# First layer of a two-block model on one core: projections in pairs of seven products, angles on GpSimd

## The reference, cut to what matters

```
hn = rmsnorm(x, norm_g)
q, k, v, u, z_a, z_b = split(hn @ w_in)            # each 1024 wide
o_a = chunked_relpos_attention(q, k, v, rel_bias) * silu(z_a)     # 16 heads of 64
y   = gelu(s5_ssm(u, ...))        # diagonal complex recurrence: a rotation by an angle and a decay
o_b = y * sigmoid(y @ w_glu + b_glu) * silu(z_b)
x   = x + concat(o_a, o_b) @ w_out
```

## Time and profile before

| | |
|---|---|
| median of 3 runs | 2581.97 us (2581.15 to 2583.98) |
| the profiled execution | 2580.91 us, its span 2579.2 us |
| busy: PE, PE weight load, DVE, ACT, POOL | 99%, 95%, 67%, 24%, 13% |
| loop of the first layer, with its start and the gate matrix behind it | the first 420 us |

### The profile page before, as it was taken

The page is one execution under the profiler, slowest core; times in us unless marked ns, Lnnn a source line. Parts: engine busy times, 40 slices in busy tenths (PEclk is TensorE's granted clock), DMA queues, the critical chain, the costliest instruction groups (busy, mean ns, idle before and its releaser), DMA issues.

```text
span 2579.2 us, 57925 instructions
## 1 busy us (share of the span) xinstructions
PE 2553.5 (99%) x22218; PEld 2458.9 (95%) x22218; DVE 1720.6 (67%) x3630; ACT 612.3 (24%) x1557; POOL 341.5 (13%) x479
## 2 busy tenths in 40 slices
PE   8999999999999999999999999999999999999998
PEld 7888889989999999999999999999999999999997
DVE  7667667565555556788998954655655655777855
ACT  3222221121001112234334320211211012344311
POOL 0111110010001100143443410211220000000000
PEclk9999999999999999999999999999999999999999
DMA  6444433444444444434334435343343444444443
GB/s 255 146 146 138 142 135 130 166 144 168 167 159 149 160 163 164 163 132 163 150 143 163 150 119 197 134 162 132 131 144 151 163 170 172 169 157 164 178 164 114
DMA packets 63764, 400.71 MB, mean 155 GB/s; under 512 B 6816, under 2 KB 13488, under 8 KB 17584
## 3 DMA queue, kind: packets, MB, share of 16 engines
q1 hardware_dynamic: 62992, 397.20, 41.8%
q0 software_dynamic: 672, 2.11, 0.5%
HBM read 397.17 MB, written 2.11 MB: 155 GB/s over the span
## 4 chain that ended last, share of the span: by engine, by line
PE 94%; DVE 3%; issue 2%; ACT 1%; DVEq 0%; DMA 0%; POOL 0%; SPq 0%; ACTq 0%; POOLq 0%
PE psum L607 68%; PE psum L551 12%; PE psum L560 2%; PE psum L1085 1%; PE psum L582 1%; PE psum L778 1%; PE psum L1094 1%; PE psum L690 1%; PE psum L871 1%; PE psum L988 1%; PE psum L842 1%; PE psum L1046 1%; PE psum L683 0%; PE psum L592 0%; PE psum L718 0%
## 5 line engine op out<-in xcount | busy, mean ns | idle before, releaser
L607 PE MATMUL psum<-h,ring 128*128 128x128 f32 x4384 | 524.3, 275 | 1.9 <-DVE near L1797 1.9
L607 PEld LDWEIGHTS psum<-h,ring 128*128 128x128 f32 x4384 | 506.6, 192 | 2.4 <-DVE wide_c L2304 2.0
L607 PE MATMUL psum<-mix,ring 128*128 128x128 f32 x3994 | 477.7, 275 | 0.4
L607 PEld LDWEIGHTS psum<-mix,ring 128*128 128x128 f32 x3994 | 461.4, 192 | 1.4 <-DVE near L1790 1.3
L551 PE MATMUL psum<-h,ring 128*128 128x256 f32 x1504 | 336.1, 381 | 0.0
L551 PEld LDWEIGHTS psum<-h,ring 128*128 128x128 f32 x1504 | 281.7, 190 | 45.7 <-issue 9.4
L1797 DVE TENSOR_TENSOR near<-psum,near 128x128 f32<-128x128 f32 x143 | 41.3, 289 | 344.9 <-PE psum L607 344.9
L607 PE MATMUL psum<-ring,h 128*128 128x128 f32 x1296 | 153.8, 275 | 0.6 <-DVE near L1797 0.6
L607 PEld LDWEIGHTS psum<-ring,h 128*128 128x128 f32 x1296 | 149.1, 192 | 0.7 <-issue 0.7
L1757 DVE TENSOR_TENSOR ring<-ring 128x1024 f32<-128x1024 f32 x112 | 137.9, 1231 | 0.0
L1154 ACT ACTIVATE w<-psum 128x128 f32<-128x128 f32 x75 | 20.8, 277 | 469.8 <-PE psum L607 469.8
(11 more groups left out here) (494 smaller groups left out, 4029.9 us busy)
## 6 DMA issues: line engine op xcount, KB each, us to landing
ring<-w_out SPq DMA_DIRECT2D x80, 1024.0 KB, 5.1
ring<-w_odd SPq DMA_DIRECT2D x64, 1024.0 KB, 4.9
ring<-w_hgrn SPq DMA_DIRECT2D x64, 1024.0 KB, 5.4
ring<-w_even SPq DMA_DIRECT2D x48, 1024.0 KB, 4.8
ring<-w_nsa SPq DMA_DIRECT2D x48, 1024.0 KB, 5.5
ring<-w_rg SPq DMA_DIRECT2D x40, 1024.0 KB, 5.4
ring<-w_cmp_in SPq DMA_DIRECT2D x8, 1024.0 KB, 4.8
ring<-w_rgg SPq DMA_DIRECT2D x10, 512.0 KB, 6.9
```

The lines of the kernel that those rows point to most:

```text
L607: mm = pe.matmul(dst, stationary, moving, start=new and j == 0, stop=new and j == kh - 1, skip_group_check=not new)
```

## The change

It touches the first layer's loop alone.

- **PE.** q with k, and z_a with z_b, become two pairs in seven products (`fast_e`), u and v stay whole. In turn 0 only the gates are such a pair; q and k are whole products there (`from_x`), taken from the raw input and scaled afterwards by DVE. The order of a turn is u (first half), the values' weighting of the turn before, u (second half), pair q/k with the read-outs of the turn before behind its first product and the drives behind its second, pair z_a/z_b with the scores behind its second product and the first head's turning behind its sixth, the second head's turning, v.
- **Banks.** The pairs take banks 0, 1, 2. u goes to bank 2, v to bank 1, drives and heads from bank 2 to bank 7, and the read-outs from bank 7 into the upper half of bank 5. So the read-outs now wait for `o_used` of their turn as well, DVE's read of the attention output in bank 5.
- **DVE** gets per turn eight forms and ten additions, and gives up the angles, the small inputs and the skip product. The forms of q/k for the next turn are made at the turn's end, behind `states(3)`. The four sums of activations are made once, into x, which is loaded again (2 MB) while the gate matrix runs.
- **POOL** gets the small inputs, the skip product (u times a column), a factor of 8 on the bias, and the angles of the next turn, between its parts of state 1 and of state 2. The angle formula uses wide_b's lower half only (its upper half now holds a form) and has one instruction more.
- **ACT** gets four reads of banks instead of four copies, the sines now stand at the turn's start and the gelu's tanh inside the q/k pair.
- **Loads.** The weights of v go to slot 10, a part of mix; z_a and z_b to slots 3 and 4.

The loop of POOL, new:

```diff
+            def angles(turn, seen):
+                y = wide_b[:, 0:4, :]
+                arg = wide_a[:, :, :].rearrange("p (t c) n -> p t c n", c=2)
+                st.mark(g.tensor_copy(cur[:, 8:12], s5[:, 1, ds(4 * turn, 4)]))
+                g.wait_ge(trig_ready, after(seen))
+                st.settle()
+                apart(g)
                 for t in range(4):
-                    g.wait_ge(rot_used, after(4 * i + t + 1))
-                    g.wait_ge(y_ready, after(4 * i))
-                    g.tensor_tensor(states5(t, 0), w8[:, 0, :], w9[:, 1, :], ALU.add).then_inc(state_ready, 1)
-                    g.tensor_tensor(states5(t, 1), w9[:, 0, :], w8[:, 1, :], ALU.subtract).then_inc(state_ready, 1)
+                    st.mark(g.tensor_scalar(y[:, t, :], ccol("time"), cur[:, 8 + t:9 + t], None, ALU.mult))
+                st.settle()
+                apart(g)
+                st.mark(g.tensor_scalar(arg[:, :, 0, :], y, ROUND, -ROUND, ALU.add, ALU.add))
+                st.mark(g.tensor_scalar(arg[:, :, 1, :], y, 0.25, ROUND, ALU.add, ALU.add))
+                st.settle()
+                st.mark(g.tensor_tensor(arg[:, :, 0, :], y, arg[:, :, 0, :], ALU.subtract))
+                st.mark(g.tensor_scalar(arg[:, :, 1, :], arg[:, :, 1, :], -ROUND, None, ALU.add))
+                st.settle()
+                g.tensor_tensor(arg[:, :, 1, :], arg[:, :, 1, :], y, ALU.subtract).then_inc(phase_ready, 1)
+            def state(i, t):
+                g.wait_ge(rot_used, after(4 * i + t + 1))
+                g.wait_ge(y_ready, after(4 * i))
+                g.tensor_tensor(states5(t, 0), w8[:, 0, :], w9[:, 1, :], ALU.add).then_inc(state_ready, 1)
+                g.tensor_tensor(states5(t, 1), w9[:, 0, :], w8[:, 1, :], ALU.subtract).then_inc(state_ready, 1)
+            def turn_inputs(i):
+                g.wait_ge(landed[6], even1.loads[3].land0 + i * even1.loads[3].land_per)
+                st.mark(g.tensor_copy(cur[:, 12:20].rearrange("p (c t) -> p c t", c=2), s5[:, 2:4, ds(4 * i, 4)]))
+                st.mark(g.tensor_copy(slope[:, 0:1], pcol("d_skip")[:, ds(i, 1)]))
+                bias = ring[:, 6, 512:1024]
+                st.mark(g.tensor_scalar(bias, bias, 8.0, None, ALU.mult))
+                st.settle()
+                apart(g)
+                st.mark(g.memset(ring[0:64, 6, 512 + 192:768], NEG))
+                g.memset(ring[0:64, 6, 768 + 192:1024], NEG).then_inc(bias_masked, 1)
+                c_mat = ring[:, 6, T:2 * T].rearrange("p (c t n) -> p c t n", c=2, t=4)
+                coef = cur[:, 12:20].rearrange("p (c t) -> p c t", c=2)
+                for n, (part, by) in enumerate(((0, 0), (1, 1), (0, 1), (1, 0))):
+                    st.mark(g.tensor_tensor(c_tmp[:, n, :].rearrange("p (t n) -> p t n", t=4), c_mat[:, part],
+                                            coef[:, by, :].unsqueeze(2).to_broadcast([P, 4, 32]), ALU.mult))
+                g.wait_ge(u_ready, after(i + 1))
+                g.wait_ge(y_used, after(i))
+                st.settle()
+                apart(g)
+                g.tensor_scalar(skip[:, :], uT[:, :], slope[:, 0:1], None, ALU.mult).then_inc(skip_made, 1)
+                st.mark(g.tensor_tensor(c_in[:, 0, :], c_tmp[:, 0, :], c_tmp[:, 1, :], ALU.subtract))
+                g.tensor_tensor(c_in[:, 1, :], c_tmp[:, 2, :], c_tmp[:, 3, :], ALU.add).then_inc(c_in_ready, 1)
+            def even_turn(i, last):
+                turn_inputs(i)
+                state(i, 0)
+                state(i, 1)
+                if not last:
+                    angles(i + 1, i + 1)
+                state(i, 2)
+                state(i, 3)
             g.wait_ge(con_in, 16)
+            g.wait_ge(s5_made, after(1))
+            angles(0, 0)
+            with g.Fori(0, PAIRS - 1) as i:
+                st.enter(i, 18)
+                even_turn(i, False)
+                st.leave(PAIRS - 1)
+            even_turn(PAIRS - 1, True)
             g.wait_ge(cum_made, after(1))
```

The turn of PE, new:

```diff
+            def gate_pair_and_values(i):
+                block_products(fast_e, i, 1, of_h, sums_even, 4, None, ((u_ready, after(i + 1)),),
+                               ((2, lambda: scores(i)), (6, lambda: turn_head(i, 0))))
+                turn_head(i, 1)
+                pe.wait_ge(later_read, after(5 * fast_e.number(i, 1) + 4))
+                values(even1, i, 6, bank[1])
+            def even_turn(i):
+                pe.wait_ge(later_read, after(5 * fast_e.number(i, 0)))
+                product(even1, i, 0, bank[2], 0, 8)
+                mix_values(i - 1)
+                product(even1, i, 0, bank[2], 8, KT)
+                block_products(fast_e, i, 0, of_h, sums_even, 4, None, ((v_ready, after(i)),),
+                               ((1, lambda: read_outs(i - 1)), (2, lambda: drives(i))))
+                gate_pair_and_values(i)
             def glu_block(b, k0, k1):
...
-            pair(PAIRS - 1, True)
+            unscaled(lambda k: tile(even1, 0, k), bank[2][:, 0:T], raw, 0)
+            from_x(even1, 1, bank[0], 6)
+            from_x(even1, 2, bank[1], 1)
+            drives(0)
+            pe.wait_ge(h_ready, after(KT))
+            gate_pair_and_values(0)
+            with pe.Fori(1, PAIRS) as i:
+                even_turn(i)
+            last = PAIRS - 1
+            pe.wait_ge(y_mixed, after(last))
+            pe.wait_ge(first_read, after(2 * EVEN))
+            wait_load(pe, glu, 0, 0)
+            glu_block(0, 0, 7)
+            mix_values(last)
+            glu_block(1, 0, 7)
+            read_outs(last)
+            pe.wait_ge(bu_used, after(4 * PAIRS))
+            wait_load(pe, glu, 0, 1)
```

What PE's hooks hold, and the slots:

```diff
+            def read_outs(i):
+                pe.wait_ge(c_in_ready, after(i + 1))
+                pe.wait_ge(y_used, after(i))
+                pe.wait_ge(o_used, after(i + 1))
+                pe.wait_ge(state_ready, after(8 * i + 8))
+                for c in range(2):
...
-        even1 = Phase(PAIRS, 6, [Load(n, tiles("w_even1", n), SLOT, n + 1) for n in range(4)] +
-                      [Load(6, None, 0, 6, 2)] +
-                      [Load(n, tiles("w_even1", n), SLOT, n + 1) for n in range(4, 6)])
+        even1 = Phase(PAIRS, 16, [Load(0, tiles("w_even1", 0), SLOT, 1), Load(1, tiles("w_even1", 1), SLOT, 7),
+                                  Load(2, tiles("w_even1", 2), SLOT, 8), Load(6, None, 0, 16, 2),
...
+        fast_e = Fast(even1, ((1, 2, None), (4, 5, None)), 8, 0, True, 1)
...
+            if ph is glu:
+                sp.wait_ge(used, done(even1, PAIRS - 1, 15))
+                sp.dma_start(x[:, :, :], a["xT"].rearrange("k p t -> p k t")).then_inc(x_back, 16)
```

The turn of DVE, new, cut to its order (`states` is unchanged but for a wait on the sines at its start; its last two products still wait for POOL's half of the state before, `v.wait_ge(state_ready, after(8 * i + 2 * t))`):

```diff
+            def even_turn(i, first, last):
+                then(v.tensor_copy(cur[:, 0:4], s5[:, 0, ds(4 * i, 4)]))
+                if not first:
+                    first_sum(fast_e, i, 0)
+                states(i, 0)
+                if not first:
+                    two_sums(fast_e, i, 0, q_and_k)
+                    three_forms(fast_e, i, 1)
+                    fourth_sum(fast_e, i, 0, q_and_k)
+                    fifth_sum(fast_e, i, 0, q_and_k)
+                states(i, 1)
+                first_sum(fast_e, i, 1)
                 v.wait_ge(bias_masked, after(i + 1))
...
+                fourth_form(fast_e, i, 1)
+                two_sums(fast_e, i, 1, z_in)
...
+                fourth_sum(fast_e, i, 1, z_in)
+                states(i, 2)
+                fifth_sum(fast_e, i, 1, z_in)
+                states(i, 3)
+                if not last:
+                    three_forms(fast_e, i + 1, 0)
                 v.wait_ge(za_tanh, after(i + 1))
...
+                if not last:
+                    fourth_form(fast_e, i + 1, 0)
                 v.wait_ge(za_used, after(i + 1))
                 v.wait_ge(o_ready, after(i + 1))
...
                 v.wait_ge(y_ready, after(4 * i + 4))
+                v.wait_ge(skip_made, after(i + 1))
+                v.tensor_tensor(w4[:, 0, :], bank[5][:, T:2 * T], skip[:, :], ALU.add).then_inc(y_used, 1)
...
+            for n, (unit, sem, times) in enumerate(((7, first_read, 2), (8, later_read, 5))):
+                v.wait_ge(used, done(even1, 0, unit))
+                v.tensor_tensor(q_and_k[:, n, :], bank[n][:, 0:T], rstd[:, :], ALU.mult).then_inc(sem, times)
+            v.wait_ge(h_ready, after(KT))
+            sums(sums_even, h[:, 0:8, :], h[:, 8:16, :], 0, made=even_sums)
+            v.sem_inc(forms_made, 2)
+            three_forms(fast_e, 0, 1)
+            even_turn(0, True, False)
+            with v.Fori(1, PAIRS - 1) as i:
+                st.enter(i - 1, 38)
+                even_turn(i, False, False)
+                st.leave(PAIRS - 2)
+            even_turn(PAIRS - 1, False, True)
```

More of the change, by code:

```diff
@@ L26 @@
 PAIRS = 8
+EVEN = 2 * PAIRS
 HEADS = 16
@@ L509, in fill @@
                         sp.wait_ge(used, ld.free0)
+                    elif ld.slot == 10:
+                        sp.wait_ge(sum_ready, after(1))
                 else:
```

(26 more changed lines are left out.)

298 lines of the change are left out of this document (121 added, 177 removed).

## The result

The changed kernel takes 2637.2 us (median; 2636.7 to 2638.6), the kernel before 2581.8 (2581.2 to 2584.0): ratio 1.0214, 95% interval 1.0196 to 1.0232. The forecast was 2634, its range 2575 to 2660, with slower at 0.71.

A forecast was written before the change was run, and what follows sets the result against it. PE bounds the loop now; the turn becomes 45.3 undisturbed + 8.7 holds - 1.0 = 53.0 us through POOL's angles. The end, 88.6 + 318.0 + 65.2 + 1.0 = 472.8 against 420.1, adds 52.7: 2634 us, range 2575 to 2660.

The forecast's parts named there:

- the 1.0 that it took off for the scans: In the loop's turn: half of the 1.9 us of holds involving DVE's scans, whose part in blocking no row showed.
- read-outs to the end of `states(1)`: First stretch of a steady turn, on DVE: 18.6 us undisturbed, 20.3 in the forecast's column.
- angles, with what POOL waits for DVE: POOL's angle operations between its states 1 and 2: 16.5 us undisturbed, 20.4 in the forecast's column.
- the POOL operation with two immediates: Operation on 1024 elements in POOL's angles, without a direct row: priced at 2.7 us, bounds 2.0 to 3.3.
- rival 5: PE's waits before read-outs halve its clock, on top of the forecast: turn 55, 2646 us, up to 2659; chance 0.13.
- the 7.7 that the forecast added: Mutual holds of DVE and POOL in a turn: 8.7 us less 1.0 for scans, added to the undisturbed 45.3.
- rival 3: Half the exclusion between POOL and DVE in the loop: turn 49 us, time 2606 us; chance 0.15.
- Waits of 5.7, 4.3 and 0.9: PE's waits in turn 0 for DVE's sums and forms, for `states(1)`, and for `first_sum`: 10.9 us lost once.
- R7 + 65.2: Start of the output projection: 65.2 us of remaining PE work and y chain after the last in-loop read-outs, R7.
- PE's pace: POOL's angles under 15.1 us and nothing long excluded, so PE sets the turn: 43.9 us, time 2571; chance 0.15.
- pairs could not bring more than 10.5 us: Whole change at best: PE's turn of 43.9 us, less turn 0's losses, ends 10.5 us sooner.
- POOL's chain without holds: Chain through POOL's angles sets the turn without exclusion between POOL and DVE: 45.3 us, time 2581; chance 0.14.

The follow-up runs named there:

- e6: e1 with the angles' two differences on POOL replaced by one-tensor products with a constant, so angles are not computed: 2593.6 us.
- e7: Changed kernel with POOL keeping the angles' products and roundings, DVE making the two differences, and turn 0's sums and forms ahead of q/k reads: 2588.4 us.
- e3: Changed kernel with 14 needless matmuls a turn on PE ahead of the read-outs, to keep it busy: 2627.1 us.
- e2: Changed kernel without the angles of turns 1 to 7, turn 0's sines being taken again: 2581.8 us.
- e9: e2 with turn 0's sums and forms ahead of the q/k reads, and the first q/k sum inside the y chain: 2575.2 us.
- e11: e7 with the second rounding behind POOL's state 1 and the first q/k sum inside the y chain: 2584.1 us.
- e12: Kernel before with only the angles moved to POOL between its states 1 and 2, and an early signal that the constants are made: 2609.2 us.
- e1: Changed kernel with the same angle operations on POOL split into three groups between its states: 2600.1 us.

## Why the prediction was right

**The turn, by its steps.** Forecast 53.0, measured 53.3 (turn 1 alone 53.6). The sum is right and its parts are not. In the forecast's column the 1.0 that it took off for the scans is taken off the angles.

| step | forecast | turn 1 of the trace |
|---|---|---|
| read-outs to the end of `states(1)` | 20.3 | 111.5 - 89.7 = 21.8 |
| POOL's state 1 | 1.45 | 112.95 - 111.5 = 1.45 |
| angles, with what POOL waits for DVE | 20.4 | 133.33 - 112.95 = 20.4 |
| to the next read-outs | 10.85 | 143.3 - 133.3 = 10.0 |

The term mis-sized inside the angles is the POOL operation with two immediates, put at 2.7 with bounds of 2.0 to 3.3: it takes 3.65, above the upper bound, so two add 1.9. The ten operations and the gaps between them take 19.2 us undisturbed (3.65 + 3.65 + 3.65 + 2.35 + 2.77 + 2.35, the cursor 0.2 and gaps of 0.6), 2.7 more than the 16.5; and POOL waited for DVE 20.4 - 19.2 = 1.2 us, not 3.9. These two errors cancel. I had both hold each other for their whole lengths, and a one-tensor POOL operation does not (e6). The first step is longer mostly by the half clock (rival 5): the product behind the read-outs takes 3.78 us (2.66 to 3.79 in the other turns), where e7's takes 2.05. The forecast took 53.0 for the case without the clock, and 55 with it; the measured figure without it is 51.8 (e3), with it 53.3.

So the direction and the path were right, and the closeness of the number is luck. The chain that nobody disturbs is 45.3 + 2.7 = 48.0. What e3 has above it, the holds and everything else, is 3.8, half of the 7.7 that the forecast added. That is the size of rival 3, half the exclusion, which I gave 0.15, though not for its reason: it is the one-tensor operations that hardly hold. Its turn of 49 comes up to the measured one only through the 2.7 of longer angles and the 1.5 of half clock, and neither was in the forecast's sum.

**Turn 0.** Waits of 5.7, 4.3 and 0.9 were forecast, together 10.9. The trace has 1.4 ahead of the drives, 5.1 and 2.7, together 9.2, and R1 is 89.7 for 88.6. This nearness too hides two errors. DVE's `states(1)` ends at 58.2 and not at 55.9, and from there to R1 it is 31.5 us and not 32.7. And without angles R1 was to be 81.0, but in e2 it is 85.3 although the waits are only 8.2: the forecast's turn 0 has no term for the half clock behind them.

**The end.** R7 + 65.2 forecast with 1.0 more for turn 7, 475.4 - 409.7 = 65.7 measured. No wait of PE for the second load of x shows behind 470 us, as said.

**The rivals.** PE's pace (2571) and POOL's chain without holds (2581) needed angles under 15.1 us or no holds; the angles take 19.2 undisturbed, and the holds were there. That pairs could not bring more than 10.5 us was right, and e9 finds 6.3 in place of it. What the trace was to show, it showed in the main: read-outs (and so drives) 53 us apart, PE's longest wait ahead of the read-outs for DVE's output, DVE's last products 5 us behind POOL's third state, POOL's operations on 1024 elements at 2.3 to 4.0 us, scans of 1.27 at 4.11. Two signs came out smaller: DVE's differences of 0.42 us were stretched to 1.36 at most and not to over 2, and PE stood still for 4.4 to 6.7 us ahead of the read-outs, not for the 9 of rival 5.

**Where it was only argued.** That a one-tensor POOL operation frees DVE behind its start rests on lengths of operations, the same in every turn of the changed kernel and of e7; why it does so is not shown. Whether PE's gaps of 0.7 us a turn at group changes are semaphores or issue was not tried.

## What to carry to other kernels

Before work moves to an idle engine, ask which chain it will stand in: the 20 us of angles a turn cost 55 us between two states that another engine waits for, 18 spread between them, in one program of seven such turns with the same operations. An engine with 88% of its time free is slow as well as free: what took DVE 5.2 us took POOL 20.4. And count the turn of the engine that feeds the saved one: seven products for eight save PE 3 us a turn and give DVE nine more operations a pair, four of them of 1024 elements; with the angles on top DVE is busy for 92% of the turn (e11), and PE waits for it 1.2 us in each.

## What the runs showed of the hardware

- A POOL operation with two SBUF tensors holds DVE's operations on two SBUF tensors to its end, scans with one column operand too: 4.11 us for 1.27 here, 3.40 in e12. The prediction had left a scan's part open at 0 or all; it is all. POOL is held too: a rounding of 3.65 us took 4.61 in e1 beside DVE's forms. The Trainium skill, "SBUF — State Buffer", section "Who interferes with whom", says that a DVE instruction with two SBUF inputs contends with a GpSimd one that reads SBUF. By that rule alone the one-tensor operations should hold too. The trace disagrees: 0.42, 0.42, 1.27 and 0.69 us unstretched under a one-tensor operation of 3.65 us, and up to 0.8 us lost only around its start.
- A DVE operation on 128 by 2 numbers with one tensor in, 0.17 us alone, took 0.73 and 1.74 beside two-tensor POOL operations (e1). The same section of the Trainium skill names `tensor_scalar` among the operations that can take the pair of ports that DVE shares with GpSimd; these lengths agree with that, but no run here shows which port was used.
- On POOL, 128 by 1024: one scalar operation 2.77 us in turn 0, two (add, add) 3.65, two tensors 2.35. Two tensors are cheaper there than one tensor with a constant.
- TensorE's granted clock was 0.50 (1.2 GHz) in the 2.4 us behind a wait of 6.6 us, 0.82 in the next 2 us and 1.00 after that. Behind the wait of 4.4 us at R1 it was 0.50 for 4.4 us. With waits of at most 0.6 us (e3) it stayed at 1.00.
